# A mixture-of-experts decoder step: the last four experts added straight to the tokens, and ranks' rows read inside the weight stream

## The reference

```python
def _moe(h, w_router, b_router, w_gu, b_gu, w_dn, b_dn):
    logits = jnp.dot(h, w_router, ...) + b_router
    top_v, top_e = lax.top_k(logits, TOP_K)
    gate = jax.nn.softmax(top_v, axis=-1)
    ...
    def expert_block(args):
        xe, e = args
        gu = xe @ w_gu[e] + b_gu[e]
        gt, up = jnp.split(gu, 2, axis=-1)
        gt = jnp.minimum(gt, SWIGLU_LIMIT)
        up = jnp.clip(up, -SWIGLU_LIMIT, SWIGLU_LIMIT)
        act = gt * jax.nn.sigmoid(SWIGLU_ALPHA * gt) * (up + 1.0)
        return act @ w_dn[e] + b_dn[e]
    ...
    y = jax.ops.segment_sum(out * slot_w[:, None], slot_tok, num_segments=t + 1)
    return y[:t]

x = x + _moe(_rmsnorm(x, norm_ffn), ...)
y = _rmsnorm(x, norm_final)
```

## Time and profile before

| | us |
|---|---|
| median of 3 runs | 1381.16 |
| lowest, highest | 1380.03, 1383.54 |
| the profiled execution | 1382.76 |
| its span in the profile | 1381.0 |
| TensorE busy | 1280.9 (93%) |
| VectorE busy | 451.7 (33%) |
| ScalarE busy | 239.9 (17%) |
| POOL busy | 118.0 (9%) |
| moved by DMA | 480.64 MB |

### The profile page before, as it was taken

One profiled execution on the slowest core, in us unless ns is written; L12 is line 12 of the kernel. 1 busy time (PEld: TensorE's weight loads), 2 busy tenths in 40 slices (PEclk: granted clock), 3 DMA queues, 4 the chain that ended last, 5 costly groups with the idle time before them and its releaser, 6 DMA issues.

```text
span 1381.0 us, 14519 instructions
## 1 busy us (share of the span) xinstructions
PE 1280.9 (93%) x5975; PEld 581.1 (42%) x5975; DVE 451.7 (33%) x800; ACT 239.9 (17%) x345; POOL 118.0 (9%) x152
## 2 busy tenths in 40 slices
PE   6999999999999999999999999999988777787885
PEld 5665776666463333333333333333322222232231
DVE  1699221211255242222222224222242222233325
ACT  3202343320112120111111111101111111111112
POOL 1110100000001110101000000101001100000020
PEclk9999999999999999999999999999999999999999
DMA  9613643452779999999999999999999999999994
GB/s 337 241 61 122 242 163 130 175 215 90 289 277 392 424 425 426 427 427 425 425 427 425 428 425 426 425 427 425 423 426 426 425 425 426 425 426 426 426 394 152
DMA packets 63621, 480.64 MB, mean 348 GB/s; under 512 B 10921, under 2 KB 11049, under 8 KB 38825
## 3 DMA queue, kind: packets, MB, share of 16 engines
q1 hardware_dynamic: 50863, 460.67, 80.7%
q0 software_dynamic: 10672, 15.39, 3.2%
q10 hardware_dynamic: 1994, 3.25, 0.7%
HBM read 478.52 MB, written 22.61 MB: 363 GB/s over the span
## 4 chain that ended last, share of the span: by engine, by line
PE 68%; DMA 29%; DVE 1%; issue 1%; ACT 1%; SPq 0%; POOL 0%; DVEq 0%; ACTq 0%
PE PS L1740 26%; PE PS L1378 15%; DMA ring<-in_w_gu 13%; PE PS L1773 12%; DMA ring<-in_w_dn 10%; PE PS L1324 4%; PE PS L1563 4%; PE PS L1606 3%; DMA ring<-y_rows 3%; DMA arena<-in_w_dn 2%; PE PS L1402 2%; DMA ring<-in_w_in 1%; DMA ring<-in_cache_mem_v 1%; PE PS L1649 0%; DVE XX L1305 0%
## 5 line engine op out<-in xcount | busy, mean ns | idle before, releaser
L1740 PE MATMUL PS<-ring,arena 128*64 128x512 f32 x1824 | 408.0, 600 | 36.4 <-DMA ring<-in_w_gu 28.9
L1235 DVE TENSOR_TENSOR arena<-PS,XX 128x1024 f32<-128x1024 f32 x32 | 39.2, 1224 | 658.6 <-PE PS L1740 658.6
L1740 PEld LDWEIGHTS PS<-ring,arena 128*64 128x64 f32 x1824 | 128.6, 139 | 293.9 <-issue 292.6
L1773 PE MATMUL PS<-ring,arena 128*64 128x512 f32 x896 | 202.3, 600 | 19.6 <-DMA ring<-in_w_dn 18.9
L1378 PE MATMUL PS<-arena,ring 128*128 128x320 f32 x768 | 216.5, 439 | 3.2 <-DMA ring<-in_w_in 3.2
L1378 PEld LDWEIGHTS PS<-arena,ring 128*128 128x128 f32 x768 | 146.2, 193 | 63.5 <-issue 7.7
L1740 PE MATMUL PS<-arena 128*64 128x512 f32 x608 | 136.2, 595 | 13.4 <-DMA arena<-in_w_gu 12.7
L851 ACT ACTIVATE arena<-arena 128x1024 f32<-128x1024 f32 x32 | 33.8, 1058 | 617.2 <-DVE arena L1238 617.2
L533 POOL DMA_INDIRECT y_rows<-arena x60 | 59.7, 995 | 789.5 <-ACT arena L832 753.9
L1773 PEld LDWEIGHTS PS<-ring,arena 128*64 128x64 f32 x896 | 62.6, 138 | 143.2 <-issue 142.2
L1324 PEld LDWEIGHTS PS<-ident,arena 128*128 128x128 f32 (+4 forms) x596 | 64.4, 141 | 54.9 <-issue 50.3
(11 more groups left out here) (206 smaller groups left out, 706.8 us busy)
## 6 DMA issues: line engine op xcount, KB each, us to landing
ring<-in_w_gu SPq DMA_DIRECT2D x96, 2048.0 KB, 27.8
ring<-in_w_dn SPq DMA_DIRECT2D x48, 2048.0 KB, 29.0
arena<-in_w_gu SPq DMA_DIRECT2D x31, 2048.0 KB, 28.2
arena<-in_w_dn SPq DMA_DIRECT2D x16, 2048.0 KB, 30.5
ring<-in_w_in SPq DMA_DIRECT2D x12, 2048.0 KB, 12.9
ring<-in_w_mem_kv SPq DMA_DIRECT2D x2, 2048.0 KB, 20.1
ring<-in_cache_mem_k SPq DMA_DIRECT2D x4, 1024.0 KB, 12.5
ring<-in_cache_mem_v SPq DMA_DIRECT2D x4, 1024.0 KB, 14.2
```

What stands on the lines that cost most here:

```text
L1235: nc.vector.tensor_tensor(gbuf[:], PS[:, 0:2, :], g_bias, ALU.add).then_inc(main["g_added"], 1)
L1740: last = mm(PS[64 * h:64 * h + 64, 2 * g + b, :], in_block(xT[:, k, :], b), (spare[kk] if m == BONUS else moe_ring(m, 2)[:, kk]) [:, g * D ...
L1773: last = mm(PS[64 * h:64 * h + 64, 4 + b, :], actT[:, b, j, c * BLK:(c + 1) * BLK], moe_ring(m, 4)[:, j, h * 512:(h + 1) * 512], start=c = ...
```

## The change

`DIRECT` becomes the last four experts, 28 to 31. The one-hot matrices are made without gates, one expert at a time (`one_hot`). Each direct expert's tile sums stand in PSUM alone, and VectorE applies the gate when it adds them to `X` (`add_tokens`). Gated biases are turned under expert 28 and summed to the tokens under expert 29. Expert 28's tiles are summed between the gate/up chunks of expert 30, expert 29's between those of expert 31, expert 30's around the first down chunk of expert 31, expert 31's at the end. For experts 28 and 29 there are only two PSUM banks, so each tile waits until VectorE has read the one before.

The rank rows become four entries of `STREAM`, behind expert 30's last gate/up chunk. SyncE reads them, once 28 experts are scattered, into four ring slots, and the chunks that come next in these slots wait for VectorE's sums (`summed`). VectorE adds all four ranks behind the activation of expert 30. All of `y_rows` is zeroed, 5.24 MB in place of 2.62. Experts 28 to 31 aren't scattered where no expert has over 128 tokens. The end no longer stands in a branch on TensorE.

```diff
+DIRECT = range(NE - 4, NE)
+_at = STREAM.index((NE - 2, 3)) + 1
+STREAM[_at:_at] = [(NE, r) for r in range(TOPK)]
...
-                sp.dma_start(y_rows[2 * T:4 * T, :].rearrange("(p j) c -> p (j c)", p=P).rearrange("p (n c) -> p n c", c=512),
-                             W[0].rearrange("p b t -> p (b t)")[:, None, 0:512].to_broadcast([P, 10, 512])) \
+                sp.dma_start(y_rows.rearrange("(p j) c -> p (j c)", p=P).rearrange("p (n c) -> p n c", c=512),
+                             W[0].rearrange("p b t -> p (b t)")[:, None, 0:512].to_broadcast([P, 20, 512])) \
...
         for i in range(RING, len(RINGED)):
-            free(0, RINGED[before_it(i)])
-            expert_chunk(RINGED[i]).then_inc(moe_loaded(RINGED[i]), 16)
+            m = RINGED[i]
+            free(0, RINGED[before_it(0, i)])
+            if is_rank(m):
+                sp.wait_ge(main["scattered"], 32 * DIRECT[0])
+                rank_rows(STREAM[m][1])
+            else:
+                expert_chunk(m).then_inc(moe_loaded(m), 16)
...
-                if e == NE - 1 and v == 0:
-                    if direct:
-                        move_weights(1, 1)
-                        move_weights(0, 2)
-                    act.wait_ge(gt_done, 1)
-                    nc.scalar.activation(GT[0:2 * NE, :], PS[0:2 * NE, 7, 0:T], ACT.Copy).then_inc(gt_ready, 1)
+                if v == 0 and e == DIRECT[0]:
+                    move_gates()
+                if v == 0 and e - 2 in DIRECT:
+                    move_weights(e - 2)
                 act.wait_ge(main["g_ready"], NE * v + e + 1)
                 nc.scalar.activation(sbuf[:], gbuf[:], ACT.Sigmoid, scale=ALPHA).then_inc(main["sig_done"], 1)
                 if 0 < e < NE - 1:
                     move_tokens(v, e + 1)
+                elif e and v == 0:
+                    move_weights(NE - 2)
+                    move_weights(NE - 1)
...
+                if v == 0 and e == DIRECT[3]:
+                    add_tokens(DIRECT[1], main["summed"], 2 + TOPK)
+                    one_hot(NE - 1)
                 dve.wait_ge(main["spread_ready"], n)
                 dve.wait_ge(main["gu_done"], n)
...
+                if v == 0 and e == DIRECT[2]:
+                    for r in range(TOPK):
+                        add_rank(r, 1, main["summed"], 2 + r)
...
+        def turn_hot(t):
+            pe.wait_ge(hot_made, t - DIRECT[0] + 1)
+            if t + 2 < NE:
+                pe.wait_ge(main["zs_ready"], t + 1)
+            elif t + 1 < NE:
+                pe.wait_ge(main["actT_ready"], NE - 1)
+            else:
+                pe.wait_ge(w_copied, t - DIRECT[0])
...
+        def to_tokens(t, tt):
+            r = ROWS[tt]
+            count = slots_used(0, t)
...
+            with pe.If(count > BLK):
+                products(0, False)
+                products(1, True).then_inc(main["tokens_done"], 1)
+            with pe.Else():
+                products(0, True).then_inc(main["tokens_done"], 1)
...
                 elif v == 0:
-                    turn_gates()
+                    turn_hot(NE - 2)
+                    turn_hot(NE - 1)
...
+        def last_experts():
+            t = NE - 2
             pe.wait_ge(main["gu_read"], NE)
-            bias_sum(0, False)
-            bias_sum(1, False)
-            turn_act(0, NE - 1)
...
+            pe.wait_ge(main["zs_ready"], NE - 1)
+            to_tokens(t, 0)
+            to_tokens(t, 1)
             pe.wait_ge(main["actT_ready"], NE)
+            down(0, NE - 1, lambda: to_tokens(t, 2))
             pe.wait_ge(main["zs_ready"], NE)
             for tt in range(TT):
-                to_tokens(1, tt).then_inc(bd_done, 1)
+                sums_read(4 + TOPK, tt)
+                to_tokens(NE - 1, tt)
```

324 lines of the change are left out of this document (170 added, 154 removed).

## The result

The changed kernel takes 1402.37 us (median of 4, 1394.72 to 1404.86) against 1382.35 us for the kernel before beside it (1380.03 to 1388.43): a ratio of 1.014, 95% interval 1.0107 to 1.0172. The direction was forecast, the size was not: 1389.2 us was forecast, and 1393.0 was the upper end. The profiled execution is the quickest of the four, 1394.72 us with a span of 1393.0.

The account below looks back on a forecast made before the run. Weight DMA bounds the kernel up to expert 31's gate/up chunks. G 1343.3 + 33.8 + 11.9 = 1389.0 against a span of 1381.0, + 8.0, so 1389.2 us as median; range 1382.5 to 1393.0.

Parts of the forecast that it names:

- Zeroing costs nothing: At the table's zero write: the second 2.62 MB need 6.4 us, covered by 7 us of pause in the queue.
- Term 1: Ranks queued ahead of expert 29's down chunks: 12.8 us at 410 GB/s, moving expert 31's gate/up end 12.0 later.
- G: End of expert 31's gate/up products on TensorE: 1331.3 in the kernel before, forecast at 1343.3.
- The slow bound, 332: If SyncE's rank rows move at 332 GB/s instead of 410, expert 31's gate/up products end 3.0 us later.
- Two rates for two issuing queues: Rank rows from POOL showed 332 GB/s, SyncE's 4 KB rows 410; 410 was taken, 332 for both adds 3.0 us.
- Term 2: From expert 31's gate/up end to the first last add: 33.8 us against 37.6, waits becoming TensorE's own chain.
- F: First add of the tile sums that only norm and output follow: 1368.96 in the kernel before, forecast at G + 33.8.
- the W copy: ScalarE copies expert 30's W behind expert 31's sigmoid, ending at G + 8.0; TensorE idles 5.3 us for it.
- Term 3: From the first of the last adds to the span's end, with norms and output: 11.9 us against 12.0.
- VectorE's jump: Jump over untaken blocks, between expert 30's third tile and F: covered, charged nothing; about 1 us if cover fails.
- The stream doesn't run dry: Weight chunks waiting for rank slots: SyncE's queue gets shorter but keeps about 15 us to spare.
- the rival with a dry stream: Rank slots freed too late, stream dry before expert 31's third chunk: about 1395 us, chance 0.04.

Follow-up runs that it names:

- zero_half: Changed kernel with only half of the table zeroed, as in the kernel before; 1402.32 us, ratio 1.0154.
- rank_tiny: Changed kernel with each rank read moving 64 bytes of each row instead of 4 KB; 1381.81 us, ratio 1.0000.
- rank_spread: Changed kernel with each rank's third tile written as 128 partitions of 2 KB instead of 64 of 4 KB; 1388.86 us, ratio 1.0053.
- before_back: Kernel before with each rank's third tile read as 128 plain rows and added from partitions 64 to 127; 1378.58 us, ratio 0.9983.
- rank_hi: w_first with the 64 rows of each rank's third tile written to partitions 64 to 127 instead of 0 to 63; 1391.77 us, ratio 1.0068.
- w_first: Changed kernel with ScalarE copying the last two W matrices before expert 31's sigmoid instead of behind it; 1390.03 us, ratio 1.0066.
- again: The changed kernel, unchanged, run once more; 1401.34 us, ratio 1.0139, traced span 1402.3.
- rank_even: Changed kernel with each rank's 64-row third tile written to partitions 0, 2, ..., 126 instead of 0 to 63; 1391.44 us, ratio 1.0071.
- "back" versions: Third tiles read as 128 plain rows, on w_first (1385.94 us), on w_first with ranks later in the stream (1380.44) and on the kernel before (1378.58).
- back_w: w_first with each rank's third tile read as 128 plain rows and added from partitions 64 to 127; 1385.94 us, ratio 1.0033.

## Why the prediction was right or wrong

- **Zeroing costs nothing:** right. Its landing takes 5.4 us more, and zero_half shows no gain.
- **Term 1, where G goes:** the step that failed. It charged 12.8 us for the ranks' 5.24 MB, and they cost 18.9 or more (rank_tiny). That they delay expert 29's down chunks, and G with them, is right. The rate isn't. I took 410 GB/s from a row "of the same shape and queue", but that row had no transfer of 64 rows in it. The slow bound, 332, came from rows in which such transfers were mixed with others, and with almost nothing but ranks in flight it is 261 to 312. In the frame of a clean seam the forecast G is 1343.3 - 4.6 = 1338.7. rank_spread, whose ranks do move at full rate, has 1335.34 + 3.66 = 1339.0. After has 1346.7. So the slow packets cost 7.7 us, and the rest of term 1 was right to 0.3, in part by luck: I let the four chunks follow at the pace of their landings, 5.0 each, but behind its wait TensorE never waits for a landing again, and its own work (4.65 to 5.15 a chunk, plus 1.5 of half clock in after and 2.4 in rank_spread) happens to take as long.
- **Two rates for two issuing queues:** misread. I put 410 to SyncE and left open whether 332 was POOL's rate. before_back issues from POOL and moves 408 between 1335 and 1345, rank_hi from SyncE 272. So it is the shape, and the trace agrees with the Trainium skill's rule after all (DMA: Bandwidth & Descriptors, "Issuing engines are not separate DMA queues").
- **Term 2, G to F:** right, 34.6 against 33.8. VectorE's late start is 3.2 (3.2 forecast), the W copy ends at G + 7.8 (8.0), the wait is 5.24 (5.3). The half clock costs 2.1 (2.5): 1.2 in the transposes and 0.9 in the chunks. The two counter reads take 1.23 and 0.95 (1380.11 less the move-out's end at 1379.16) instead of 0.5 each, together 1.2 more; with 0.4 less for the clock that is the missing 0.8. w_first takes 6.5 out again, so this is the price of putting the copies behind the sigmoid, as said. My reason for the half clock, an idle time longer than the harmless 3.02, was thinner than I wrote. The trace of before has a shorter one that was not harmless, 5.15 for a chunk of 3.65:

```profile
1334.02 5.15 PE L1773 MATMUL PS<-ring,arena 128*64 128x512 f32 x16 [2.68 <-DMA ring<-in_w_dn]
```

- **Term 3, the tail:** right, 11.7 against 11.9; VectorE's jump stayed covered.
- **The stream doesn't run dry:** right. No wait for gate/up chunks of expert 31 shows in after, and the rival with a dry stream didn't come about. Its number, 1395, lies near the trace for another reason.
- **The ground under the sum:** the second error, and not in any step. The profiled execution of before was 4.6 us late at the seam, and this went into the sum as if it belonged to the kernel. On the traces: 1389.0 - 4.6 (seam) + 7.7 (packets) + 0.8 - 0.2 = 1392.7 against 1393.0. On the medians: the profiled run of after is 7.7 under its median, and again's trace is 8.8 late at the seam, so most of the way to 1402 is probably the seam; only one of those executions has a trace.

What stays open is why the changed kernel meets a late seam so often. Of the 17 traces of it and its variants 9 are clean, 7 late with half clock, and one (rank_tiny) 1.4 late at full clock; of before and its variants 1 of 3 is clean. w_first's median lies 12.3 under after's though its clean trace lies only 6.7 under. The instructions ahead of the seam are the same in after and w_first, and zero_half has the half clock without the larger write. I didn't find what decides it.

## What to carry to other kernels

Before a price per byte is taken from another transfer, its partitions and outermost dimension must be compared, not only its row size and its queue: here 64 rows into one half of the partitions slowed the traffic beside them, and it paid to read 128 plain rows, 20% more bytes, and add from the upper half. A copy that TensorE waits for belongs ahead of the long chain on its engine, since the wait also cost the half clock behind it (2.1 of 6.5 us here). And two traces should be aligned at a point ahead of the change before their later rows are subtracted.

## What the runs showed of the hardware

- 64 rows of 4 KB to partitions 0 to 63, or 64 to 127, take the 4 KB packets of a stretch from 168 to 314 ns at the 90th percentile and the weights' 16 KB packets from 620 to 995 (rank_even against after); the same 64 rows to every second partition don't. The busy share shows 1.02 at 261 GB/s all the same, so a full busy share doesn't mean a full rate.
- VectorE adds two SBUF tiles whose partitions differ by 64 (the third tiles of the "back" versions): the sums of three ranks, nine instructions of which three are of this kind, took 11.43 us in back_w where they took 10.83 in after, so 3.8 a rank instead of 3.6.
- SyncE stands in issue instructions for 8 to 10 us when ranks are queued, with 64 bytes a row as much as with 4 KB (7.84 and 9.41 in rank_tiny, 7.80 and 9.46 after). So the ranks' own bytes don't set it; whether it is their number of rows or what is queued ahead of them, no run separates.
- Half clock at the same place of a program comes and goes from one execution to the next of the same kernel (1.00 from 390 to 395 in after, 0.50 in again), and cost about 8 us there (8.8 late at the gather, 0.7 of it from before).
- The length of TensorE's idle time alone doesn't tell whether half clock follows: in before a chunk took 5.15 us behind 2.68 of idle time, and 3.65 behind 3.02.
